# Ten modulation pieces summed during the even projection, by VectorE and GpSimd, instead of six by VectorE alone

## The chip, the core and the metric

The kernel runs on one core of a Trainium2 chip. The core has five engines, each with its own program: TensorE (PE in the profile, its weight loads PEld), VectorE (DVE), ScalarE (ACT), GpSimd (POOL) and SyncE (SP, which here only issues DMAs). They meet through semaphores: an instruction raises one when it is done, and another engine's program waits until it has reached a value. The metric is the device time of one execution in microseconds.

## The reference

The model is a two-layer backbone over 1024 latent tokens and 256 context tokens, with 1024 channels, all in float32. An even layer runs grouped-query attention beside a bidirectional mLSTM, an odd layer two other kinds of attention; both are followed by a mixture of 32 experts. Each layer is modulated by vectors that come from the conditioning vector alone:

```
mod_l = silu(c)     @ w_ada[layer] + b_ada[layer]      # six vectors of 1024 for latent tokens
mod_c = silu(c_ctx) @ w_ada[layer] + b_ada[layer]      # six for context tokens
sh1, sc1, g1, sh2, sc2, g2 = split(mod_l, 6)
h = rms_norm(x, g_mix[layer]) * (1 + sc1) + sh1        # what the mixer reads
```

`w_ada` is 1024 x 6144 for each of two layers, 48 MB together. The kernel cuts it into 24 pieces of 512 columns (1024 rows x 512 columns, 2 MB). A piece is a weighted sum over the rows: 8 row blocks of 128 rows, each scaled by its rows' values of silu(c) (kind 0) or silu(c_ctx) (kind 1), added up, and then summed over the 128 partitions.

## The kernel before, in words

The stages run one after the other: modulation, even projection, mLSTM, even attention, output projection, experts of layer 0, and the same for the odd layer. The 24 pieces of the modulation are spread over these stages.

- Pieces 0 to 3 (`EARLY`) are computed in the modulation stage on PE, since the projection needs them.
- Pieces 4 to 9 (`SUMMED = 6`, L145) are scaled and added over the row blocks by DVE during the even projection, for both kinds. What comes out (128 partitions x 512 columns for each piece and kind) goes to DRAM (`g.sum_dram`).
- The mLSTM stage begins with `units` (L765). A unit "sums" reads up to four of these from DRAM, and PE sums them over the partitions with the selecting matrix `sel`; a unit "whole" loads one of the pieces 10 to 15 (2 MB) and PE does the whole product (`ada_product`, L157). Four buffers take turns (`wa`, `buf`, L774), and eight units (`LATE`, L775) go through load, `product`, `ada_out` on ACT, and `turn`. The mLSTM's loop starts when all are through.
- Pieces 16 to 23 (`LAST`) are scaled and added by POOL during the even attention, for kind 0 alone: a `tensor_scalar` with a column of `g.cs` (L1309) and a `tensor_tensor` add (L1317) for each row block.

**The even projection (L366).** Ten tiles of 128 tokens, tile number 2i + h. `walk_tiles` unrolls the first and the last pair; the others run in a loop on each engine (DVE has its own loop of `SUMMED // 2 - 1` turns, then unrolled tiles). For a tile, PE does rows 0 and 1, `turn_qk` of the tile before, rows 2, `transposes` of the tile after, rows 3, and `channels`. `turn_qk` (L499) waits for `x_sq`, ACT's squares of the tile two further on, and for `z_dve`, DVE's `channels_out` of the tile. `transposes` (L459) waits for `xh_ready`, DVE's normalised tokens, and for `qt_dve`, DVE's `k_out`.

DVE does, in the order of its program (L699): the first half of a piece's sum (`summed`, half 0), `rows_out`, `k_out` of the tile before, `norm_rope`, `modulate` for the next tile, the second half of the sum, `channels_out`, and `normalise` for the tile two further on. `channels_out` and `modulate` read PSUM; `summed`, `norm_rope` and `normalise` read and write SBUF.

The weights for the sums come in `slabs`, one piece of two halves (4 row blocks, 1 MB each), which lies in the last 512 columns of `zT`; `acc`, two accumulators, lies in the last 512 columns of `qT`. Both places get their real contents only from tile 6 on, so ACT waits for the sums before it writes there (L579, L589). A half is loaded again when DVE is done with it (`slab_used`). SP issues these loads, the loads of the tokens (`x_load`, which waits for the transposes of an earlier tile) and the stores of the sums in one queue, in the order of L428 to L441.

POOL's program in this stage fills `y_dram`, the experts' output, with zeros: four DMAs of 4.6 MB (L451), issued when the input weights are in, and then a wait until they have landed.

Of the kernel before, what the change touches and what calls it, by code (L numbers as in the profile page):

```python
# [25 lines left out]
ALU = mybir.AluOpType  # L26
# [3 lines left out]
P = 128  # L30
# [3 lines left out]
T = SEQ + CTX  # L34
# [37 lines left out]
class Count:  # L72
# [11 lines left out]

    def but(self, n):

        return self.sem, self.base + self.k - n

    def turn(self, i, per):
# [54 lines left out]
LAST = range(NCHUNK - 8, NCHUNK)  # L144
SUMMED = 6  # L145

# [219 lines left out]
def even_project(nc, g, A, L):  # L366
# [5 lines left out]
    with nc.cleanup_on_exit():  # L372
# [19 lines left out]
        def s(name):  # L392
            return nc.alloc_semaphore("ep_" + name)
# [9 lines left out]
        slabs = L.zT[:, :, T - 512:T]  # L403
        acc = [L.qT[:, kind, T - 512:T] for kind in range(2)]
        slab_in, slab_used = [s("slab_in0"), s("slab_in1")], [s("slab_used0"), s("slab_used1")]
        acc_st = s("acc_st")
        c = Count(nc, "ep_dve_step")
        with nc.Block() as block:

            @block.sync  # L410
            def _(sp):
                def x_load(n):

                    sp.wait_ge(t_done, 2 * n + 2)
                    sp.dma_start(x[:, n % 2, :], A["x"][0, n * P:(n + 1) * P, :]).then_inc(x_in[n % 2], 16)

                def slab_load(n, half):
                    if n:
                        sp.wait_ge(slab_used[half], n)
                    col = (EARLY + n) * 512  # L420
                    sp.dma_start(slabs[:, 4 * half:4 * half + 4, :],
                                 A["w_ada"][0, half * 512:(half + 1) * 512, col:col + 512].rearrange("(k p) n -> p k n", p=P)).then_inc(slab_in[half], 16)

                def acc_store(n):
                    sp.wait_ge(slab_used[1], n + 1)
                    sp.dma_start(g.sum_dram[:, n, :, :], L.qT[:, 0:2, T - 512:T]).then_inc(acc_st, 16)
# [12 lines left out]
                for n in range(SUMMED + 2, NTL):  # L439
                    x_load(n)  # L440
                sp.wait_ge(acc_st, 16 * SUMMED)  # L441
# [12 lines left out]

# [82 lines left out]
            def _(act):  # L537
# [38 lines left out]
                def channels_out(i, h, halves=(0, 1)):  # L576

                    if h == 0 and not place_of(i, h)[0] and not place_of(i, h)[1]:
                        act.wait_ge(slab_used[1], i * 2)  # L579
                    for half in halves:  # L580
                        act.wait_ge(z_done, i * 4 + 2 * h + half + 1)
                        for cc in range(4 * half, 4 * half + 4):
                            m = act.activation(L.zT[:, cc, bass.ds(i * 256 + h * P, P)], ps_ab[:, h, half, (cc % 4) * P:(cc % 4) * P + P], ACT.Identity,
                                               scale=L.halfw[:, cc + 8:cc + 9], bias=L.halfw[:, cc + 24:cc + 25])
                        m.then_inc(z_act, 1)

                def q_out(i, h):
                    if h == 0 and not place_of(i, h)[0] and not place_of(i, h)[1]:
                        act.wait_ge(acc_st, i * 32)  # L589
# [31 lines left out]
            def _(dve):  # L621
# [54 lines left out]

                def summed(i, h, half):

                    n = i * 2 + h - 1
                    dve.wait_ge(slab_in[half], n * 16 + 16)  # L680
                    if half == 0 and not (isinstance(n, int) and n == 0):
                        dve.wait_ge(acc_st, n * 16)
                    for k in range(4 * half, 4 * half + 4):
# [8 lines left out]
                    dve.wait_ge(*c.now())  # L692
                    dve.sem_inc(slab_used[half], 1)

# [4 lines left out]
                def tile(i, h):  # L699
                    first, final, last, before, after = place_of(i, h)  # L700
                    sums = not first and not (isinstance(i, int) and i * 2 + h > SUMMED)
# [25 lines left out]
                tile(0, 1)  # L727
                turns = SUMMED // 2 - 1
                with dve.Fori(0, turns) as j:
# [9 lines left out]
def even_mlstm(nc, g, A, L):  # L739
# [4 lines left out]
    def s(name):  # L744
        return nc.alloc_semaphore("ml_" + name)

    with nc.cleanup_on_exit():
# [25 lines left out]
        wa.append(arena[:, 0:KD * 512].rearrange("p (k n) -> p k n", n=512))  # L773
        buf = lambda n: n % 4  # L774
        assert LATE == 8  # L775
        wt = nc.alloc_sbuf_tensor("ml_wt", [P, 2, BH, P], F32)
# [43 lines left out]
        with nc.Block() as block:  # L820

            @block.sync
            def _(sp):
# [9 lines left out]

                for n in range(6):
                    load(n)
# [3 lines left out]
                sp.dma_start(row_dram[1].rearrange("d r t -> (d r) t"), ai_row).then_inc(rows_out, 16)  # L839
                for n in range(6, LATE):  # L840
                    load(n)
                sp.wait_ge(rows_out, 32)
# [11 lines left out]
                def body(it, step, tiles):  # L854
                    if isinstance(it, int):
                        rows_in(0, step)
                        rows_in(1, step)
                        sp.wait_ge(ada_mm, LATE - 1)
                        for b in range(4):
                            values_in(b, tiles)  # L860
                        sp.wait_ge(ada_mm, LATE)
                        rows_in(2, step)
# [11 lines left out]
            def _(pool):  # L874
# [14 lines left out]
                def body(it, step, tiles):  # L889
                    for par in range(2):  # L890
                        for d in range(2):
                            b, tile = 2 * par + d, tiles(par)[d]
                            if isinstance(it, int) and it == 0:
                                pool.wait_ge(ada_mm, LATE - 3 + par)

# [117 lines left out]
            def _(act):  # L1013
# [30 lines left out]
                for cc in range(2, 8):  # L1044
                    gate(cc)
                    if cc < 6:
                        ada_out(cc)
                for n in range(6, LATE):
                    ada_out(n)
                act.wait_ge(tabs_ready, 1)  # L1050
# [21 lines left out]
            def _(dve):  # L1072
# [82 lines left out]
                dve.wait_ge(ada_turned, LATE)  # L1155
                for a, b in ((0, 4), (4, SUMMED)):
                    to = slice(4 * (EARLY + a), 4 * (EARLY + b))
# [2102 lines left out]
```

## Time and profile before

| | us |
|---|---|
| device time, median of 3 runs | 3146.27 (3143.32 to 3149.4) |
| the profiled execution | 3146.45 |
| its span, first to last instruction | 3144.5 |
| busy: PE / DVE / ACT / POOL | 2863.3 / 1480.4 / 1082.9 / 692.9 |
| mean granted clock of PE | 0.959 |

The profile is of one execution. A row of a timeline has the start in us from the span's start, the length, the engine, the line of the kernel, the operation, output and inputs, shapes and count; in brackets stands how long the engine was idle before it and what released it. Neighbouring instructions of one line are put together (x8). A row of grouped instructions has minimum, median and maximum in ns. The whole span in 40 slices of 78.6 us, each digit the busy share in tenths, shows the even projection in the second to fifth slice and the first half of the sixth:

```profile
PE   6999988899999689999987999899999959998895
DVE  2667436755554432222224677566665342232223
POOL 0000005799051033332221010000002013332233
PEclk8999988899999899999998999899999979999998
DMA  9722027433052399999984221200003459999997
```

### The profile page before, as it was taken

The page shows a single profiled execution, that of the slowest core. Times are in us where ns is not written, and L with a number is a line of the kernel's source. Part 1 is how long each engine was busy: PE and PEld are TensorE (multiplying, and loading weights), DVE is VectorE, ACT ScalarE, POOL GpSimd, SP SyncE. Part 2 cuts the span into 40 slices and gives each one's busy share as a digit, 9 for nine tenths or more (in the row PEclk, how much of TensorE's full clock was granted, in tenths as well). Part 3 has the DMA queues.
Part 4 walks back from the last instruction along what each step waited for, and adds up shares of the span by engine and source line. Part 5 has one row for each costly group of instructions (what it writes and reads, how often), then busy time and mean ns, then how long its engine had stood idle before and what let it go on. Part 6 is the DMA issues. An engine that isn't in the chain of part 4 may idle for free. (4 is left out here: it accounts for less than half of the span.)

```text
span 3144.5 us, 72871 instructions
## 1 busy us (share of the span) xinstructions
PE 2863.3 (91%) x27771; PEld 1889.6 (60%) x27771; DVE 1480.4 (47%) x4244; ACT 1082.9 (34%) x2480; POOL 692.9 (22%) x929
## 2 busy tenths in 40 slices
PE   6999988899999689999987999899999959998895
PEld 3666656745544357776663555577776537795573
DVE  2667436755554432222224677566665342232223
ACT  1222124466621123333333343455553103332232
POOL 0000005799051033332221010000002013332233
PEclk8999988899999899999998999899999979999998
DMA  9722027433052399999984221200003459999997
GB/s 371 276 91 77 20 102 231 116 112 100 1 181 88 158 376 414 413 416 417 418 355 155 84 82 66 74 1 1 1 1 116 154 222 384 418 416 417 418 417 300
DMA packets 167397, 665.00 MB, mean 211 GB/s; under 512 B 25373, under 2 KB 37929, under 8 KB 117621
## 3 DMA queue, kind: packets, MB, share of 16 engines
q1 hardware_dynamic: 136736, 574.30, 47.1%
q0 software_dynamic: 19456, 56.67, 5.1%
q10 hardware_dynamic: 10964, 30.68, 2.5%
q8 instruction: 170, 2.79, 0.4%
q14 instruction: 71, 0.57, 0.1%
HBM read 581.98 MB, written 86.90 MB: 213 GB/s over the span
## 5 line engine op out<-in xcount | busy, mean ns | idle before, releaser
L2877 PE MATMUL ps_g<-w_ring,work 128*32 128x256 f32 x7328 | 432.0, 382 | 26.5 <-DMA w_ring<-in_w 15.1
L2964 DVE STREAM_TRANSPOSE work<-work 128x256 f32<-128x256 f32 x189 | 123.6, 654 | 662.1 <-PE ps_g L2877 633.6
L2877 PEld LDWEIGHTS ps_g<-w_ring,work 128*32 128x32 f32 x7328 | 290.7, 110 | 138.5 <-issue 32.4
L2930 ACT COPY work<-ps_y 32x256 f32<-32x256 f32 x760 | 275.7, 363 | 285.0 <-PE ps_y L2892 278.2
L2877 PE MATMUL ps_g<-w_early,work 128*32 128x256 f32 x4640 | 281.4, 389 | 36.2 <-DMA w_early<-in_w 24.7
L2002 PE MATMUL of_ps_r<-w_early,cat 128*128 128x512 f32 (+1 forms) x608 | 255.9, 577 | 1.6 <-ACT cat L2084 1.6
L2877 PEld LDWEIGHTS ps_g<-w_early,work 128*32 128x32 f32 x4640 | 183.6, 112 | 113.3 <-issue 44.8
L484 PE MATMUL ps_r<-w,hT 128*128 128x512 f32 (+1 forms) x640 | 250.0, 547 | 1.5 <-ACT hT L554 1.5
L2825 POOL DMA_INDIRECT work<-f_dram,ex_idx x200 | 204.6, 1023 | 171.4 <-POOL ex_idx L2822 168.9
L2924 ACT ACTIVATE work<-ps_g 128x128 f32<-128x128 f32 x192 | 53.3, 277 | 515.8 <-PE ps_g L2877 509.1
L2892 PE MATMUL ps_y<-w_ring,work 128*32 128x256 f32 x3680 | 226.7, 380 | 3.4 <-ACT work L2930 3.4
L2833 POOL COPY work<-work 128x256 f32<-128x256 f32 x192 | 76.6, 399 | 535.7 <-DVE work L2964 395.2
L2002 PEld LDWEIGHTS of_ps_r<-w_early,cat 128*128 128x128 f32 x608 | 114.8, 192 | 124.6 <-issue 122.3
L484 PEld LDWEIGHTS ps_r<-w,hT 128*128 128x128 f32 x640 | 120.4, 192 | 114.8 <-issue 107.4
L1653 PE MATMUL mo_ps_o<-mo_w,mo_cT 128*128 128x512 f32 x416 | 185.8, 599 | 1.6 <-DMA mo_w<-in_e_w_out 0.9
L2892 PEld LDWEIGHTS ps_y<-w_ring,work 128*32 128x32 f32 x3680 | 150.1, 111 | 56.0 <-ACT work L2930 4.3
L2464 DVE TENSOR_SCALAR_CACHE_REDUCE w_early<-oa_ps_s 128x512 f32<-128x512 f32 (+1 forms) x288 | 159.0, 598 | 20.4 <-PE oa_ps_s L2378 17.8
L2433 ACT ACTIVATE w_early<-w_early,oa_mins 128x1280 f32<-128x1280 f32 x96 | 131.0, 1364 | 65.9 <-DVE oa_mins L2470 65.9
L495 PEld LDWEIGHTS ps_ab<-hT,w 128*128 128x128 f32 x1280 | 144.6, 192 | 4.8 <-issue 4.8
L495 PE MATMUL ps_ab<-hT,w 128*128 128x128 f32 x1280 | 144.7, 275 | 0.0
L2892 PE MATMUL ps_y<-w_early,work 128*32 128x256 f32 x2304 | 141.5, 381 | 0.0
L1653 PEld LDWEIGHTS mo_ps_o<-mo_w,mo_cT 128*128 128x128 f32 x416 | 78.9, 192 | 100.5 <-issue 98.0
(509 smaller groups left out, 4432.7 us busy)
## 6 DMA issues: line engine op xcount, KB each, us to landing
w_ring<-in_w SPq DMA_DIRECT2D x232, 1024.0 KB, 25.2
w_early<-in_w SPq DMA_DIRECT2D x152, 1024.0 KB, 25.4
y_dram<-work ACTq DMA_DIRECT2D x190, 128.0 KB, 5.9
y_dram<-zeros POOLq DMA_DIRECT2D x4, 4608.0 KB, 27.2
ea_slab<-in_w_ada SPq DMA_DIRECT2D x64, 256.0 KB, 2.9
zT<-in_w_ada SPq DMA_DIRECT2D x12, 1024.0 KB, 6.0
f_dram<-mo_f SPq DMA_DIRECT2D x18, 512.0 KB, 2.9
w<-in_e_w_in SPq DMA_DIRECT2D x2, 4096.0 KB, 20.4
```

What stands on the lines that cost most here:

```text
L484: mm = pe.matmul(ps_r[:, n, 0:cols[1] - cols[0]], hT[:, h, k, :], w[:, k, cols[0]:cols[1]], start=k == 0, stop=k == KD - 1)
L495: mm = pe.matmul(ps_ab[:, h, half, (cc % 4) * P:(cc % 4) * P + P], w[:, k, Z0 + cc * P:Z0 + (cc + 1) * P], hT[:, h, k, :], start=k == 0, s ...
L1653: mm = pe.matmul(ps_o[:, half * 512:(half + 1) * 512], row, w[:, k, half * 512:(half + 1) * 512], start=k == 0, stop=k == KD - 1)
L2002: mm = pe.matmul(ps_r[:, bank[m], 0:b - a], hT[:, n % 2, k, :], w[:, k, a:b], start=k == 0, stop=k == KD - 1)
L2433: act.activation(sx[:, n % 3, part, :], sx[:, n % 3, part, :], ACT.Exp, scale=-1.0, bias=mins[:, n % 3, part, 3:4], accum_out=sums[:, n % ...
L2464: dve.tensor_scalar(sx[:, n % 3, part, a:b], ps_s[:, k % 2, part, 0:b - a], -SCALE[units[n][1]], BIG, ALU.mult, ALU.min, accum_out=mins[:, ...
L2825: pool.indirect_dma_start(out=xg[:, at * 256:(at + 1) * 256], out_offset=None, in_=R.f_dram.rearrange("t (q d) -> (t q) d", q=QU), in_offs ...
L2833: pool.tensor_copy(xs, xg[:, at * 256:(at + 1) * 256]).then_inc(x_ready, 1)
L2877: mm = pe.matmul(ps_h[rows, :], xT[:, k * UNIT:(k + 1) * UNIT], w[:, :, kk * DE + n * P:kk * DE + (n + 1) * P], start=k == 0, stop=k == KD ...
L2892: mm = pe.matmul(ps_y[n * UNIT:(n + 1) * UNIT, :], hT[:, k * UNIT:(k + 1) * UNIT], w[:, kk, n * 256:(n + 1) * 256], start=k == 0, stop=k == 3)
L2930: w = act.copy(y[b * UNIT:(b + 1) * UNIT, n * 256:(n + 1) * 256], ps_y[n * UNIT:(n + 1) * UNIT, :])
L2964: dve.transpose(xT.rearrange("p (k t) -> p k t", k=KD), xs.rearrange("p (r k) -> p k r", k=KD)).then_inc(x_turned, 1)
```

## The change

`SUMMED` becomes 10: the even projection sums pieces 4 to 13. DVE does kind 0 of each piece and POOL kind 1, from the same slab. DVE does two pieces in each of the tiles 1 to 5, one at the beginning of the tile and one before `channels_out`, with one accumulator, and so waits for its own last operation each time. [...] POOL's accumulator has two buffers. A half of the slab is loaded again when both engines are done with it. SP's order is new: the load of the next half 0, DVE's store, the load of the next half 1, POOL's store, and after every second piece a load of tokens.

The mLSTM stage has five units instead of eight: two "sums" of four pieces, two "whole" (pieces 14 and 15), one "sums" of two pieces; the waits on `ada_mm` that name units follow.

```diff
-SUMMED = 6
+SUMMED = 10
...
                 for n in range(SUMMED):
-                    if n + 1 < SUMMED:
-                        slab_load(n + 1, 0)
-                    x_load(n + 2)
-                    acc_store(n)
-                    if n + 1 < SUMMED:
-                        slab_load(n + 1, 1)
-                for n in range(SUMMED + 2, NTL):
-                    x_load(n)
+                    slab_load(n + 1, 0)
+                    dve_store(n)
+                    slab_load(n + 1, 1)
+                    pool_store(n)
+                    if n % 2 == 0:
+                        x_load(n // 2 + 2)
+                x_load(SUMMED // 2 + 2)
...
+                for n in range(SUMMED):
+                    to = acc_pool[n % 2]
+                    for half in range(2):
+                        pool.wait_ge(slab_in[half], 16 * n + 16)
+                        if half == 0 and n > 1:
+                            pool.wait_ge(pool_st[n % 2], 16 * (n // 2))
+                        for k in range(4 * half, 4 * half + 4):
+                            pool.tensor_scalar(product if k else to, slabs[:, k, :], L.cs[:, k, 1:2], None, ALU.mult).then_inc(*pool_step.up())
+                            pool.wait_ge(*pool_step.now())
+                            if k:
+                                pool.tensor_tensor(to, to, product, ALU.add).then_inc(*pool_step.up())
+                                pool.wait_ge(*pool_step.now())
+                        pool.sem_inc(used_pool[half], 1)
                 pool.wait_ge(filled, 64)
...
                 def channels_out(i, h, halves=(0, 1)):
                     if h == 0 and not place_of(i, h)[0] and not place_of(i, h)[1]:
-                        act.wait_ge(slab_used[1], i * 2)
+                        act.wait_ge(used_dve[1], i * 4 - 2)
+                        act.wait_ge(used_pool[1], i * 4 - 2)
...
-                def summed(i, h, half):
+                def summed(i, h, second):
-                    n = i * 2 + h - 1
+                    n = i * 4 + 2 * h - 2 + second
...
-                        for kind in range(2):
-                            by = L.cs[:, k, kind:kind + 1]
+                            by = L.cs[:, k, 0:1]
                             if k == 0:
-                                m = dve.tensor_scalar(acc[kind], slabs[:, k, :], by, None, ALU.mult)
+                                m = dve.tensor_scalar(acc, slabs[:, k, :], by, None, ALU.mult)
                             else:
-                                dve.wait_ge(*c.but(1))
-                                m = dve.scalar_tensor_tensor(out=acc[kind], in0=slabs[:, k, :], scalar=by, in1=acc[kind], op0=ALU.mult, op1=ALU.add)
+                                dve.wait_ge(*c.now())
+                                m = dve.scalar_tensor_tensor(out=acc, in0=slabs[:, k, :], scalar=by, in1=acc, op0=ALU.mult, op1=ALU.add)
...
-        units = [("sums", 0, 4)] + [("whole", q) for q in range(whole, whole + 3)] + [("sums", 4, SUMMED)] + [("whole", q) for q in range(whole + 3, LAST[0])]
+        units = [("sums", 0, 4), ("sums", 4, 8)] + [("whole", q) for q in range(whole, LAST[0])] + [("sums", 8, SUMMED)]
```

## Rows read from the trace of the kernel before

**Rows 1.** Busy us in 40 us: PE, PEld, DVE, ACT, POOL, clock, DMA.
```profile
152.00:192.00 40.00, 40.00 (x206) 27.78 (x205) 26.28 (x71) 7.92 (x18) 0.00 (x0) 1.00 0.28 92
```

**Rows 2.** Timeline of PE, tiles 1 and 2 of the even projection.
```profile
105.65 1.04 PE L467 MATMUL ps_ab<-consts_sb,x 128*128 128x128 f32 x8
...
138.22 0.60 PE L514 MATMUL ps_ab<-consts_sb,sq 128*128 128x128 f32 x4
...
145.63 1.04 PE L467 MATMUL ps_ab<-consts_sb,x 128*128 128x128 f32 x8
```

**Rows 3.** Timeline of DVE, tile 2 of the even projection.
```profile
140.96 0.29 DVE L697 COPY kT<-ps_ab 128x128 f32 x1
...
151.05 5.38 DVE L690 SCALAR_TENSOR_TENSOR qT<-zT,cs,qT 128x512 f32<-128x512 f32 x8
162.44 0.30 DVE L665 COPY edges<-ps_ab 128x4 f32 x2 [6.00 <-ACT zT L583]
...
163.98 1.12 DVE L673 SCALAR_TENSOR_TENSOR zT<-ps_ab,halfw,zT 128x127 f32 x4
169.60 0.29 DVE L665 COPY edges<-ps_ab 128x4 f32 x2 [4.50 <-ACT zT L583]
...
173.54 0.15 DVE L626 TENSOR_SCALAR xs<-xs 128x1 f32<-128x1 f32 x1 [1.30 <-ACT ps_ab L546]
```

**Rows 4.** Instructions on the tile zT: min/median/max ns, starts.
```profile
L690 DVE SCALAR_TENSOR_TENSOR qT<-zT,cs,qT x84: 743/748/751, 96.1 to 315.7; 128x512 f32<-128x512 f32 x84
```

**Rows 5.** Timeline of POOL, even projection: issues of the fills.
```profile
63.68 5.73 POOL L451 DMA_DIRECT2D y_dram<-zeros  x3 [21.48 <-DMA w<-in_e_w_in]
...
117.21 1.83 POOL L451 DMA_DIRECT2D y_dram<-zeros  x1 [47.80 <-issue]
```

**Rows 6.** POOL's lines L1309, L1317, L1614 (min/median/max ns), then its timeline.
```profile
L1309 POOL TENSOR_SCALAR ea_slab<-ea_slab,cs x64: 1553/1564/1579, 608.6 to 781.2; 128x512 f32<-128x512 f32 x64
...
L1317 POOL TENSOR_TENSOR ea_slab<-ea_slab x56: 1261/1272/1289, 611.8 to 782.8; 128x512 f32<-128x512 f32 x56
...
L1614 POOL TENSOR_SCALAR qT<-qT x10: 612/617/1599, 892.4 to 951.2; 128x512 f32<-128x512 f32 x10
...
618.79 1.56 POOL L1309 TENSOR_SCALAR ea_slab<-ea_slab,cs 128x512 f32<-128x512 f32 x1
620.43 1.26 POOL L1317 TENSOR_TENSOR ea_slab<-ea_slab 128x512 f32<-128x512 f32 x1
621.68 1.56 POOL L1309 TENSOR_SCALAR ea_slab<-ea_slab,cs 128x512 f32<-128x512 f32 x1
```

**Rows 7.** Timelines of POOL and DVE after the even attention.
```profile
895.47 1.29 POOL L1610 TENSOR_TENSOR hb<-hb,gbc 128x512 f32<-128x512 f32 x1
895.66 1.13 DVE L119 TENSOR_TENSOR mo_s<-mo_s,mo_ss 128x16 f32<-128x16 f32 x1
...
920.75 2.11 POOL L1616 TENSOR_TENSOR hb<-hb,qT 128x512 f32<-128x512 f32 x1
921.77 2.17 DVE L1818 TENSOR_TENSOR mo_f<-mo_f,mo_rows 128x1024 f32<-128x1024 f32 x1
```

**Rows 8.** DMA issues, 130 to 330 us: KB, median us to landing.
```profile
zT<-in_w_ada SPq DMA_DIRECT2D x8, 1024.0 KB, 5.4
```

**Rows 9.** Timelines of SP, POOL and PE, head of the mLSTM stage.
```profile
452.64 0.34 SPq L830 DMA_DIRECT2D ml_staging<-sum_dram  x1
...
485.87 3.52 SPq L848 DMA_DIRECT2D ml_spare<-ml_rows  x4
...
492.18 1.38 POOL L886 MEMSET hb<- 128x1536 f32 x1 [33.66 <-DVE zT L1078]
...
498.84 3.64 PE L157 MATMUL ml_ps_c<-ml_arena,cs 128*32 128x512 f32 x16 [3.12 <-DMA ml_arena<-in_w_ada]
...
500.30 0.20 POOL L900 COPY ml_cur<-ml_tab 128x16 f32<-128x16 f32 x1 [6.74 <-DMA ml_spare<-ml_rows]
...
505.85 2.05 PE L974 MATMUL ml_ps_s<-ml_staging 128*128 128x128 f32 x8
```

More of the change, by code:

```diff
@@ L403, in even_project @@
         slabs = L.zT[:, :, T - 512:T]
-        acc = [L.qT[:, kind, T - 512:T] for kind in range(2)]
-        slab_in, slab_used = [s("slab_in0"), s("slab_in1")], [s("slab_used0"), s("slab_used1")]
-        acc_st = s("acc_st")
+        acc, acc_pool, product = L.qT[:, 0, T - 512:T], [L.qT[:, n, T - 512:T] for n in (1, 3)], L.qT[:, 2, T - 512:T]
+        slab_in = [s("slab_in0"), s("slab_in1")]
+        used_dve, used_pool = [s("used_dve0"), s("used_dve1")], [s("used_pool0"), s("used_pool1")]
+        dve_st, pool_st = s("dve_st"), [s("pool_st0"), s("pool_st1")]
+        pool_step = Count(nc, "ep_pool_step")
         c = Count(nc, "ep_dve_step")
@@ L417, in slab_load, with dve_store, pool_store @@
                 def slab_load(n, half):
+                    if n >= SUMMED:
+                        return
                     if n:
-                        sp.wait_ge(slab_used[half], n)
-                    col = (EARLY + n) * 512
+                        sp.wait_ge(used_dve[half], n)
+                        sp.wait_ge(used_pool[half], n)
+                    layer, col = (EARLY + n) // (NCHUNK // 2), (EARLY + n) % (NCHUNK // 2) * 512
                     sp.dma_start(slabs[:, 4 * half:4 * half + 4, :],
[L422 to L426, printed above, removed]
+                                 A["w_ada"][layer, half * 512:(half + 1) * 512, col:col + 512].rearrange("(k p) n -> p k n", p=P)).then_inc(slab_in[half], 16)
+                def dve_store(n):
+                    sp.wait_ge(used_dve[1], n + 1)
+                    sp.dma_start(g.sum_dram[:, n, 0, :], acc).then_inc(dve_st, 16)
+                def pool_store(n):
+                    sp.wait_ge(used_pool[1], n + 1)
+                    sp.dma_start(g.sum_dram[:, n, 1, :], acc_pool[n % 2]).then_inc(pool_st[n % 2], 16)
                 x_load(0)
@@ L432, in _ @@
                 for n in range(SUMMED):
-                    if n + 1 < SUMMED:
-                        slab_load(n + 1, 0)
-                    x_load(n + 2)
-                    acc_store(n)
-                    if n + 1 < SUMMED:
-                        slab_load(n + 1, 1)
-                for n in range(SUMMED + 2, NTL):
-                    x_load(n)
-                sp.wait_ge(acc_st, 16 * SUMMED)
+                    slab_load(n + 1, 0)
[5 more added lines that the diff above has]
+                x_load(SUMMED // 2 + 2)
+                sp.wait_ge(dve_st, 16 * SUMMED)
+                for b in range(2):
+                    sp.wait_ge(pool_st[b], 8 * SUMMED)
             @block.gpsimd
@@ L588, in q_out @@
                     if h == 0 and not place_of(i, h)[0] and not place_of(i, h)[1]:
-                        act.wait_ge(acc_st, i * 32)
+                        act.wait_ge(dve_st, i * 64 - 32)
+                        for b in range(2):
+                            act.wait_ge(pool_st[b], i * 32 - 16)
                     act.wait_ge(qt_done, i * 2 + h + 2)
@@ L675, in channels_out @@
                         m.then_inc(z_dve, 1)
-                def summed(i, h, half):
-                    n = i * 2 + h - 1
[L680 to L683, printed above, removed]
-                        for kind in range(2):
-                            by = L.cs[:, k, kind:kind + 1]
+                def summed(i, h, second):
+                    n = i * 4 + 2 * h - 2 + second
+                    for half in range(2):
+                        dve.wait_ge(slab_in[half], n * 16 + 16)
+                        if half == 0 and not (isinstance(n, int) and n == 0):
+                            dve.wait_ge(dve_st, n * 16)
+                        for k in range(4 * half, 4 * half + 4):
+                            by = L.cs[:, k, 0:1]
                             if k == 0:
-                                m = dve.tensor_scalar(acc[kind], slabs[:, k, :], by, None, ALU.mult)
+                                m = dve.tensor_scalar(acc, slabs[:, k, :], by, None, ALU.mult)
                             else:
-                                dve.wait_ge(*c.but(1))
-                                m = dve.scalar_tensor_tensor(out=acc[kind], in0=slabs[:, k, :], scalar=by, in1=acc[kind], op0=ALU.mult, op1=ALU.add)
+                                dve.wait_ge(*c.now())
+                                m = dve.scalar_tensor_tensor(out=acc, in0=slabs[:, k, :], scalar=by, in1=acc, op0=ALU.mult, op1=ALU.add)
                             m.then_inc(*c.up())
-                    dve.wait_ge(*c.now())
-                    dve.sem_inc(slab_used[half], 1)
+                        dve.wait_ge(*c.now())
+                        dve.sem_inc(used_dve[half], 1)
                 def k_out(i, h):
@@ L700, in tile @@
                     first, final, last, before, after = place_of(i, h)
-                    sums = not first and not (isinstance(i, int) and i * 2 + h > SUMMED)
+                    sums = not first and not (isinstance(i, int) and i * 2 + h > SUMMED // 2)
                     if sums:
@@ L727, in _ @@
                 tile(0, 1)
-                turns = SUMMED // 2 - 1
+                turns = SUMMED // 4
                 with dve.Fori(0, turns) as j:
@@ L773, in even_mlstm @@
         wa.append(arena[:, 0:KD * 512].rearrange("p (k n) -> p k n", n=512))
-        buf = lambda n: n % 4
-        assert LATE == 8
+        buf = lambda n: (n + 1) % 4
+        assert LATE == 5
         wt = nc.alloc_sbuf_tensor("ml_wt", [P, 2, BH, P], F32)
@@ L832, in load @@
                         ada_load(sp, A, units[n][1], wa[buf(n)], ada_in[buf(n)])
-                for n in range(6):
+                for n in range(LATE):
                     load(n)
@@ L839, in _ @@
                 sp.dma_start(row_dram[1].rearrange("d r t -> (d r) t"), ai_row).then_inc(rows_out, 16)
-                for n in range(6, LATE):
-                    load(n)
                 sp.wait_ge(rows_out, 32)
@@ L1045, in _ @@
                     gate(cc)
-                    if cc < 6:
+                    if cc < LATE:
                         ada_out(cc)
-                for n in range(6, LATE):
-                    ada_out(n)
                 act.wait_ge(tabs_ready, 1)
@@ L1155, in _ @@
                 dve.wait_ge(ada_turned, LATE)
-                for a, b in ((0, 4), (4, SUMMED)):
+                for a, b in ((0, 4), (4, 8), (8, SUMMED)):
                     to = slice(4 * (EARLY + a), 4 * (EARLY + b))
```

8 lines of the change are left out of this document (3 added, 5 removed).

## The prediction, on record before the result

> **What bounds the kernel now.** I read the stretches of the even projection first, since most of the change is there, then the engines' timelines in them, then the place where GpSimd already does the same kind of sum, and last the head of the mLSTM stage. In a 40 us stretch of the projection PE is busy all 40.00 us at a granted clock of 1.00, DVE 26.28 us, POOL not at all, and the DMA engines 0.28 of the time [rows 1]. A token tile takes 40.0 us: the transposes (L467) of one tile begin at 105.65, of the next at 145.63 [rows 2]. So PE is the bound there, and whatever PE has to wait is added to the end. PE waits for DVE at two places in a tile: `turn_qk` (L503) wants the squares of a later tile, which come after DVE's `channels_out`, and `transposes` wants DVE's `k_out` of the tile before, which stands right behind the first sum. Today `k_out` is done at 141.2, 4.4 us early, and DVE has slack: in a tile it waits 6.00, 4.50 and 1.30 us for ACT [rows 3].
>
> The head of the mLSTM stage is bound otherwise: PE's last product waits for its slab until 498.84, POOL's first staging copy waits until 500.30 for table rows that queue behind the slabs, and the first scores begin at 505.85, 53 us after the stage's first load at 452.64 [rows 9].
>
> **POOL's new work.** Ten pieces, each of 8 multiplies and 7 adds of 128x512, every one waiting for the one before. The same two instructions stand in the even attention: the multiply by a column of `cs` takes 1.56 us (64 of them, 1553 to 1579 ns), the add 1.27 us. A dependent add starts 1.64 us after its multiply, and the following multiply, which does not depend on it, 1.25 us after the add [rows 6]. With a wait after every instruction I take 1.64 and 1.33 (the same 0.08 us for the wait). Half a slab is then 4 x 1.64 + 3 x 1.33 = 10.6 us and the second half 4 x 2.97 = 11.9 us: 22.4 us a piece, 44.9 us for the two pieces of a tile, against 40.0 us of PE. POOL alone is thus too slow already.
>
> It also starts late. POOL first issues the four fills of `y_dram`; three go out from 63.68, but the fourth only at 117.21 for 1.83 us [rows 5], so the first multiply can't start before 119.0 (perhaps 115, if the fill drains faster with one slab load fewer beside it).
>
> **What both engines cost each other.** Where POOL and DVE work on SBUF together (the gate products after the even attention), they take turns. DVE's L1818 is issued at 921.77 and ends at 923.94, and POOL's L1616, issued at 920.75, ends at 922.86: each runs after the other's end, POOL's in 2.11 instead of 1.27 us. From the end of L1616 to the end of L1818 is 1.08 us for 1024 columns. A small DVE operation, L119, takes 1.13 us, though it has only 16 columns: it ends just after POOL's L1610, which had begun before it [rows 7]. The new sums are two-input SBUF operations like L1818, and so are nearly all of `norm_rope`. So I take it that they exclude each other. [...]
>
> DVE's own path through a tile: 40.0 less its waits (11.8) and plus 1.3 for the squares is 29.5 us. The sums in it are two eights of 5.38 us, 10.8; with one accumulator instead of two each of the 16 must wait for the one before, 0.75 + 0.04 = 0.79 us, 12.6 in all [rows 3, 4]. That makes 31.3 us. POOL adds 16 x 1.56 + 14 x 1.27 = 42.8 us of instructions. I take it that POOL can run without holding DVE while DVE reads PSUM (in the attention, where DVE does, POOL's rows hardly vary [rows 6]) or waits for ACT: `channels_out` some 5 (each half like 162.44 to 165.1), the squares 1.3, `modulate` about 1.1 (four operations, as L673's), `rows_out`, `k_out` and the reduction some 1.8, in all 9.2 us. An instruction that has waited for the other engine has its start behind it (1.13 after the hand-over instead of 1.27; on DVE 0.54 for 512 columns instead of 0.75): 30 x 0.14 and about 12 x 0.2, together 6.6 us. The tile becomes 31.3 + 42.8 - 9.2 - 6.6 = 58.3 us, 18.3 more than PE needs. Without exclusion it would be POOL's 44.9, and with no overlap at all 74; I take 58, which the rows of taking turns give.
>
> **The first tiles, step by step.** DVE sums piece 0 from 96 [rows 4], but piece 1 needs the slab back. POOL ends the first half of piece 0 at 129.6; the load of 1 MB lands 5.4 us later [rows 8], 135.0. POOL ends the second half at 141.5, and 2.2 us later since DVE's first four operations fall into it: 143.7; that load lands at 149.1. DVE's piece 1 ends at 156.4, `channels_out` at 161.3, the squares at 162.6, the normalising (2.3 us, and two POOL instructions, 4.9) at 167.5. Then piece 2, eight operations that each let one POOL instruction pass, 8 x (0.54 + 1.28) = 14.6, and `k_out`: 182.9. PE's transposes were at 145.63, so they are 37 us late. In the next tile both pieces run against POOL for their whole length, 64.7 us, then come two tiles of 58.3: 24.7 + 36.6 = 61 us more. After the last of these `k_out`, DVE still needs some 38 us to the squares (58.3 less 14.6 for the sum, 0.8, and 4.9 for the normalising), PE from its transposes to `turn_qk` 32.6 (105.65 to 138.22 [rows 2]): 5.5 us beyond that. The projection becomes longer by 37 + 61 + 5.5 = 104 us, with bounds of 42 and 142 from the rivals below. PE stands still for some microseconds before it goes on; after the last such wait I add 2 us for a lower clock, an estimate: half of the 3.64 us of the product at 498.84, which runs right after a wait [rows 9].
>
> **Other edits.** SP's order: `x_load` now stands behind `pool_store`, and so behind POOL, which puts the load of tile 4's tokens at about 144; they are read after two more tiles, some 80 us later, so nothing. Queued behind SP's waits are only the next slab halves, which wait for the same POOL. The slab traffic grows from 12 to 20 MB and the stores from 3 to 5 MB: the DMA engines were at 0.28 [rows 1], so nothing; were they full, 8 MB would cost some 20 us. ACT's new waits before `channels_out` and `q_out` ask for pieces that POOL ends 10 us or more earlier: nothing. POOL's wait for the fill now stands behind the sums: nothing.
>
> **The head of the mLSTM stage.** Five units instead of eight, 9 MB instead of 15. The slabs are there some 18 us earlier. Next late is the chain of gates on ACT and DVE, which loses one `ada_out` (0.6 us and its wait): about 2 us earlier, so POOL's clearing at 492.18 comes at 490.2 and ends at 491.6. The table rows, issued at 485.87 because their stores queued behind slabs, come at about 482 and land with nothing ahead of them before 490. So POOL stages from 491.6 instead of 500.30, and PE, no longer turning the last piece until 505.85, follows after 3.8 us, at 495.4: 10 us gained [rows 9]. Bounds: 2 (the gates alone) and 18 (all that the slabs free).
>
> **Sum.** The profiled execution took 3146.45 us (its span 3144.5), 0.2 from the median of the three runs, 3146.27. 3146.45 + 104 + 2 - 10 = 3242 us.
>
> **Rivals.** First, the engines don't exclude each other in these forms and POOL alone is the bound. Then DVE's piece 8 ends 119.0 + 8 x 22.4 + 5.4 + 3.2, and `k_out` 0.8 later at 307.6, against 265.6 (145.63 and three tiles): +42, less 10: 3179 us. For it: the 64 multiplies of the attention hardly vary though DVE is busy beside them. Against it: that DVE reads PSUM there, and rows 7.
>
> Second, the turns cost full price and each piece shows a slab landing: 31.3 + 42.8 - 9.2 + 6 = 71 us a tile, 37 + 3 x 31 + 12 = 142, in all 3146 + 142 - 10 = 3278 us. For it: small operations on DVE may each wait for a whole POOL instruction, and a tile has some 20.
>
> Third, on the other side: POOL's piece is cheap enough to hide. The multiply with two immediates (L1614) takes 617 ns [rows 6]; at that price a piece is 8 x 0.62 + 7 x 1.27 = 13.9 us, and without exclusion only the late start is left, 119.0 + 2 x 13.9 + 9.4 - 145.6 = 10.6 us. With the full 18 us at the mLSTM head this gives 3139 us. It decides at about 17 us a piece, where the later tiles would begin to wait. [...] Against it too: exclusion would add to every piece.
>
> **How the numbers follow.** The forecast 0.70, its own range 3210 to 3270 by the start at 115 or 119 and by 54 to 64 us a tile; the first rival 0.10, the second 0.14, the third 0.04, and a sum of such parts that comes to nothing 0.02. The range 3175 to 3290 takes in the first two rivals. What can be told from no change here is 0.2%, about 6 us: slower 0.94, within it 0.02, faster 0.04.
>
> **What would show it.** Right: PE idle before L467 and `turn_qk` in four or five tiles of the projection, tiles of 55 to 65 us there, DVE's L690 at well above 0.75 us, POOL's new adds above 1.27 us, the mLSTM stage beginning near 558 instead of 452.6, and some 43 us from there to the first scores. POOL's multiplies at 1.56 us with tiles of 45 us would show the first rival, multiplies near 0.6 us and no idle PE the third. The prediction is wrong if DVE's sums keep 0.75 us beside POOL, or if POOL starts long before 115.

## The result and the profile after

The changed kernel takes 3200.56 us (median of 4 runs, 3199.02 to 3204.45) against 3147.84 us (4 runs, 3143.32 to 3149.56): ratio 1.0171, 95% interval 1.0159 to 1.0183, or 52.7 us more. The prediction had the sign and the place, and 96 us. The measured time lies in its range of 3175 to 3290, but below the 3210 to 3270 of the forecast itself. The profiled execution is the longest of the four, 3204.45 us (span 3202.7).

PE in the even projection of the changed kernel (start, length; in brackets the idle time before and who ended it) answers to [rows 2]; the line of the transposes is now L486:

```profile
103.20 1.04 PE L486 MATMUL ps_ab<-consts_sb,x 128*128 128x128 f32 x8
...
153.88 1.11 PE L533 MATMUL ps_ab<-consts_sb,sq 128*128 128x128 f32 x4 [17.94 <-ACT ps_ab L565]
...
173.42 1.94 PE L486 MATMUL ps_ab<-consts_sb,x 128*128 128x128 f32 x8 [8.99 <-DVE kT L719]
223.90 1.94 PE L486 MATMUL ps_ab<-consts_sb,x 128*128 128x128 f32 x8 [8.60 <-DVE kT L719]
274.14 1.94 PE L486 MATMUL ps_ab<-consts_sb,x 128*128 128x128 f32 x8 [8.00 <-DVE kT L719]
324.64 1.94 PE L486 MATMUL ps_ab<-consts_sb,x 128*128 128x128 f32 x8 [7.79 <-DVE kT L719]
367.54 1.04 PE L486 MATMUL ps_ab<-consts_sb,x 128*128 128x128 f32 x8
```

Before, these transposes stood 39.98 us apart. Now the first distance is 70.2 us (30.2 late), three are 50.2 to 50.5, the next is 42.9. Next comes a stretch of 40 us, to be read beside [rows 1]. Below it stands what DVE waited for from 160 to 360 us and POOL from 100 to 400 us (us in total, times, longest):

```profile
158.00:198.00 40.00, 31.01 (x167) 22.16 (x166) 29.47 (x42) 4.71 (x12) 37.44 (x24) 0.85 0.39 126
```
```profile
DVE qT L712 <- DMA zT<-in_w_ada: 33.1, 8, 6.8
```
```profile
POOL qT L466 <- POOL qT L469: 4.4, 19, 0.3
```

POOL is busy 37.44 of 40 us and, once begun, never waits for data, only for itself, at most 0.3 us at a time. DVE waits 33.1 us in eight waits, 4 us each, for the next half of a slab, which is loaded when POOL lets go of the old one. So in these tiles POOL is the bound, not DVE. Its instructions and DVE's sums (min, median, max in ns; beside [rows 6] and [rows 4]):

```profile
L466 POOL TENSOR_SCALAR qT<-zT,cs x80: 1562/1568/2014, 114.5 to 360.6; 128x512 f32<-128x512 f32 x80
...
L469 POOL TENSOR_TENSOR qT<-qT x70: 1259/1270/1867, 117.9 to 362.2; 128x512 f32<-128x512 f32 x70
...
L712 DVE SCALAR_TENSOR_TENSOR qT<-zT,cs,qT x70: 750/1059/1643, 93.4 to 348.2; 128x512 f32<-128x512 f32 x70
```

The mLSTM stage begins at 514.66 instead of 452.64 (+62.0); to the first scores it takes 44.65 us instead of 53.21 [rows 9]:

```profile
514.66 0.32 SPq L852 DMA_DIRECT2D ml_staging<-sum_dram  x1
```
```profile
559.31 2.08 PE L994 MATMUL ml_ps_s<-ml_staging 128*128 128x128 f32 x8 [9.37 <-POOL ml_staging L926]
```

62.0 - 8.6 = 53.4 us, which accounts for the 52.7 between the medians. The two profiled executions lie 58.0 us apart; the other 4.7 us come after the first scores. Runs of one kernel differ by 5 to 6 us, so I leave them unexplained.

### The profile page after: what moved, and what is told of

Its sections match the earlier page's. It is cut to its first block and busy times, and to the rows that moved or that the text cites. A ratio compares the mean times of both kernels' runs of the same rounds, so it can differ in the third digit from the quotient of the medians.

```text
span 3202.7 us, 72957 instructions
## 1 busy us (share of the span) xinstructions
PE 2874.2 (90%) x27699; PEld 1896.1 (59%) x27699; DVE 1522.4 (48%) x4229; ACT 1081.6 (34%) x2477; POOL 923.5 (29%) x1079
## 3 DMA queue, kind: packets, MB, share of 16 engines
q1 hardware_dynamic: 138192, 578.49, 46.7%
## 5 line engine op out<-in xcount | busy, mean ns | idle before, releaser
L2895 PEld LDWEIGHTS ps_g<-w_ring,work 128*32 128x32 f32 x7328 | 291.9, 111 | 137.2 <-issue 33.1
L2895 PE MATMUL ps_g<-w_early,work 128*32 128x256 f32 x4640 | 282.4, 389 | 35.1 <-DMA w_early<-in_w 23.7
L503 PE MATMUL ps_r<-w,hT 128*128 128x512 f32 (+1 forms) x640 | 257.1, 559 | 1.5 <-ACT hT L573 1.5
L2910 PEld LDWEIGHTS ps_y<-w_ring,work 128*32 128x32 f32 x3680 | 150.8, 111 | 56.5 <-issue 4.5
L1626 POOL TENSOR_TENSOR cat<-cat,mo_rs 128x512 f32<-128x512 f32 x8 | 10.4, 1306 | 481.7 <-DVEq L1811 481.7
## 6 DMA issues: line engine op xcount, KB each, us to landing
w_ring<-in_w SPq DMA_DIRECT2D x232, 1024.0 KB, 23.7
```

Source lines behind the costliest of these rows:

```text
L503: mm = pe.matmul(ps_r[:, n, 0:cols[1] - cols[0]], hT[:, h, k, :], w[:, k, cols[0]:cols[1]], start=k == 0, stop=k == KD - 1)
L2895: mm = pe.matmul(ps_h[rows, :], xT[:, k * UNIT:(k + 1) * UNIT], w[:, :, kk * DE + n * P:kk * DE + (n + 1) * P], start=k == 0, stop=k == KD ...
L2910: mm = pe.matmul(ps_y[n * UNIT:(n + 1) * UNIT, :], hT[:, k * UNIT:(k + 1) * UNIT], w[:, kk, n * 256:(n + 1) * 256], start=k == 0, stop=k == 3)
```

## The experiments

Theory A: POOL's own chain sets the pace of the tiles. Theory B, as predicted: DVE's path does, held up by the whole length of every POOL instruction. Each total is given with its ratio to the kernel before on the same chip. Runs 1, 3, 8 and 10 change values, so later stages see other values; there the start of the mLSTM stage tells more than the total.

**1. No sums on POOL.** POOL clears both accumulators and only signals.

```diff
-                        for k in range(4 * half, 4 * half + 4):
-                            pool.tensor_scalar(...) ... pool.tensor_tensor(...)
```

> The changed kernel without GpSimd's 150 multiplies and adds: GpSimd clears its two accumulators once, stores these zeros ten times and keeps all its signals. So the second row of ten pieces is zero, later stages see other values, and the starts of stages are read beside the total. Theory A (GpSimd's own chain of 22.4 us a piece, stretched to 25.1 by VectorE, sets the projection's pace) and theory B (as predicted: VectorE's own path, lengthened by the whole length of every GpSimd instruction, sets it) both expect no wait of TensorE left in the projection, mLSTM's first head product at about 453 to 456 us in place of 514.66, its head 8.6 us shorter than in the kernel before, and a total of about 3139 us. A rival C, that the larger traffic of slabs and stores or the code around the sums costs a good part of the 62 us, expects the projection to stay 10 us or more late and the total at 3150 or more.

3148.92 us (1.0003, 0.9993 to 1.0013); mLSTM begins at 464.39, +11.75. PE's transposes and DVE's second piece:

```profile
103.71 1.04 PE L483 MATMUL ps_ab<-consts_sb,x 128*128 128x128 f32 x8
...
156.89 1.07 PE L483 MATMUL ps_ab<-consts_sb,x 128*128 128x128 f32 x8 [0.33 <-DVE kT L716]
196.91 1.04 PE L483 MATMUL ps_ab<-consts_sb,x 128*128 128x128 f32 x8
```
```profile
133.57 0.48 DVE L706 TENSOR_SCALAR qT<-zT,cs 128x512 f32<-128x512 f32 x1 [23.48 <-DMA sum_dram<-qT]
```

Both theories missed 13.2 us at the third tile, which here come without any arithmetic on POOL; the later tiles are back at 40. POOL's first signal still stands behind the fills, SP's store of DVE's first piece stands behind the slab load that waits for this signal, and DVE, with one accumulator, waits for the store. That store also travels slowly, beside the last fill. SP's issues, and the stores' time to landing between 90 and 140 us and between 160 and 300 us:

```profile
115.89 0.37 SPq L422 DMA_DIRECT2D zT<-in_w_ada  x1
116.30 1.52 SPq L427 DMA_DIRECT2D sum_dram<-qT  x1
```
```profile
sum_dram<-qT SPq DMA_DIRECT2D x2, 256.0 KB, 18.1
```
```profile
sum_dram<-qT SPq DMA_DIRECT2D x14, 256.0 KB, 3.2
```

By these rows the 13.2 us have two parts, which no run separates: the signal comes at 115.9, and the store then takes 17 us instead of 3. The other 17 of the 30 us, and all growth, need POOL's sums.

**2. Fills behind the sums.** The four DMAs of `y_dram` are issued after POOL's sums.

> The changed kernel with GpSimd's four fills of the expert rows issued behind its sums in place of ahead of them: its first multiply can start about 45 us earlier (about 70 us in place of 114.53), and nothing else changes. Theory A (GpSimd's chain, 25.1 us a piece from its first instruction on): TensorE's wait of 30 us at its third tile goes nearly whole, what is left grows by some 10 us a tile as GpSimd falls behind, the projection ends about 22 to 25 us later than before in place of 62, total about 3164 us. Theory B (VectorE's path, about 50 us for each tile in which it meets GpSimd, whenever GpSimd starts): the tile after the first is now slowed as well, so 10 us are paid five times, the projection ends about 50 us late, total about 3188 us.

3167.19 us (1.0064, 1.0046 to 1.0082): A's 3164, not B's 3188. mLSTM begins at 479.68, +27.0. PE's transposes:

```profile
104.24 1.04 PE L486 MATMUL ps_ab<-consts_sb,x 128*128 128x128 f32 x8
145.41 1.06 PE L486 MATMUL ps_ab<-consts_sb,x 128*128 128x128 f32 x8 [1.02 <-DVE kT L719]
189.26 1.89 PE L486 MATMUL ps_ab<-consts_sb,x 128*128 128x128 f32 x8 [3.68 <-DVE kT L719]
239.48 1.94 PE L486 MATMUL ps_ab<-consts_sb,x 128*128 128x128 f32 x8 [8.37 <-DVE kT L719]
```

The first distance is only 1.2 us longer than before although POOL already works beside it (busy 38.44 of 41 us); POOL's lead is used up first, and then the tiles take 50 us again. The late start was worth 33 us of the loss.

**3. Constant instead of column.** `slabs[:, k, :], 0.5, None, ALU.mult`.

> The changed kernel with GpSimd's 80 multiplies by the constant 0.5 in place of a column of the condition (the second row of ten pieces has other values, so the starts of stages are read beside the total); the multiply then takes about 0.62 us (as other multiplies by constants of this tile in the trace) in place of 1.56, a piece 13.9 in place of 22.4. The fills stay ahead of the sums. Theory A: GpSimd keeps up with a tile of 40 us, so only its late start is left: +17 to +30 us at the third tile and no further growth; total about 3156 to 3169 us. Theory B by the full length of every GpSimd instruction: 27.8 us per tile hold VectorE in place of 42.8, tile 43 to 46 us, growth of 3 to 6 us a tile behind the same first delay; total about 3170 to 3185 us.

3202.02 us (1.0178, 1.0159 to 1.0197); mLSTM begins at 509.14, +56.5. The premise failed: this multiply still takes 1510 ns (median of 80), so the run tells nothing between A and B. See 9 and 10.

**4 to 6. POOL's instructions beside the kernel before.** On buffers of their own, from 120 us on, read by nobody:

```diff
+                for n in range(120):     # 4: multiplies; 5: 140 adds; 6: 64 pairs
+                    pool.tensor_scalar(pa, pc, L.cs[:, n % 8, 1:2], None, ALU.mult).then_inc(*pool_step.up())
+                    pool.wait_ge(*pool_step.now())
```

> The kernel before, with 120 multiplies by a column of the condition on GpSimd, in its own buffers, from about 119 us on (187 us of them); nothing reads them, VectorE, its six pieces and its slabs are as before. [...] Theory A' (the column multiply holds VectorE out only for about its first 0.65 of 1.56 us): VectorE's path stays near the 40 us of TensorE's tile; 0 to 8 us, total 3147 to 3156. Theory B (every GpSimd instruction holds VectorE out for its whole length): 25 us more on VectorE's path in each tile, some 17 us a tile for 4 tiles, +60 to +75, total about 3215.

> The kernel before, with 140 adds of two tiles on GpSimd (178 us of them), in its own buffers, from about 119 us on; nothing reads them. The add holds VectorE out for its whole 1.27 us by theory A' and by theory B, so both expect a clear loss: VectorE's path 48 to 56 us a tile for 3.5 to 4.5 tiles, +35 to +70 us, total 3183 to 3218. What tells A' from B is that it loses several times what the multiplies alone lose (A'), or as much (B).

> The kernel before, with 64 pairs of a column multiply and an add on GpSimd (181 us alone, some 200 with what it loses to VectorE), in its own buffers, from about 119 us on; nothing reads them. It is the changed kernel's mix of instructions without its dependences. Theory A (in the changed kernel GpSimd's own chain sets the pace, and VectorE has some 6 us a tile to spare): VectorE's path 44 us a tile, +4 us a tile, about +20 (10 to 35), total 3158 to 3183. Theory B (VectorE's path sets it): as in the changed kernel, 10 us a tile for 4 tiles at least, or by the full exclusion of the prediction 18.6 us a tile, +40 to +80, total 3188 to 3228.

Multiplies: 3147.62 us (0.9999, 0.9989 to 1.0008). Adds: 3218.89 (1.0217, 1.0200 to 1.0234). Pairs: 3161.85 (1.0036, 1.0023 to 1.0049). DVE's groups between 150 and 310 us follow (after the bar busy us and mean ns of one), with multiplies, adds and pairs. They are the sums, where both tensors lie in SBUF, and in the first two a group with one input in PSUM; with adds also the first multiply of a sum, which reads one tensor, from SBUF:

```profile
L701 DVE SCALAR_TENSOR_TENSOR qT<-zT,cs,qT 128x512 f32<-128x512 f32 x56 | 45.8, 883 | 0.0
...
L684 DVE SCALAR_TENSOR_TENSOR zT<-ps_ab,halfw,zT 128x127 f32 x32 | 9.0, 342 | 1.1
```
```profile
L701 DVE SCALAR_TENSOR_TENSOR qT<-zT,cs,qT 128x512 f32<-128x512 f32 x36 | 59.8, 1727 | 0.0
...
L698 DVE TENSOR_SCALAR qT<-zT,cs 128x512 f32<-128x512 f32 x4 | 5.7, 1465 | 1.3 <-issue 1.3
L684 DVE SCALAR_TENSOR_TENSOR zT<-ps_ab,halfw,zT 128x127 f32 x20 | 5.6, 342 | 0.7
```
```profile
L703 DVE SCALAR_TENSOR_TENSOR qT<-zT,cs,qT 128x512 f32<-128x512 f32 x50 | 56.7, 1200 | 0.0
```

A sum of 748 ns [rows 4] becomes 883 beside multiplies that run without a break and 1727 beside adds. The operations that read PSUM keep 342 ns even there. In the run with pairs, POOL's mix without its dependences, a tile takes 42.5 to 45.3 us: that is DVE's path by itself, some 6 us short of the 50 of the changed kernel. (Its sums have two accumulators; the prediction put one accumulator at 1.8 us a tile more.) B's 58.3 and its +40 to +80 are refuted by 4 and 6; A is held up.

**7 and 11. DVE alone, ten pieces.** The twenty half pieces in tiles 1 to 6 as 3, 4, 4, 4, 3, 2, two sets of accumulators; fills behind (7) or ahead (11).

```diff
+        acc = [[L.qT[:, 2 * b + kind, T - 512:T] for kind in range(2)] for b in range(2)]
+        units_of = {1: (1, 2, 0), 2: (1, 2, 1), 3: (1, 2, 1), 4: (1, 2, 1), 5: (1, 2, 0), 6: (1, 1, 0)}
...
+                    for v in range(b):
+                        summed(u + a + v)
...
+                    elif m:
+                        channels_out(i, h, (0,))
+                        summed(u + a + b)
+                        channels_out(i, h, (1,))
```

> A version that is to beat both: ten pieces, both rows by VectorE alone, GpSimd without any sum; 20 half pieces (5.4 us each in the trace of before) in tiles 1 to 6 as 3, 4, 4, 4, 3, 2 in place of 2 a tile, the further ones put where VectorE waited 6.0 us and 4.5 us for ScalarE in a tile; two sets of accumulators; the fills behind the last piece; mLSTM's head as in the changed kernel. Theory A: what cost time was GpSimd's chain and its late start, and VectorE had the room, 11.8 us of waits a tile for 5.4 to 10.8 us more of sums; TensorE waits for 0 to 6 us in the whole projection, the head of mLSTM gives 8.6 us back, total 3139 to 3145 us. Rival: a tile with four half pieces leaves VectorE no room (31.3 + 10.8 us of path against 40), some 3 us late in three tiles, and the slabs' loads come late besides; the 8.6 us are used up, total 3148 or more.

> The version with ten pieces by VectorE alone, but with the fills of the expert rows at their old place, ahead, about 64 to 117 us. It tells whether the fills' place matters where GpSimd sums nothing. Case one: the slabs' loads and stores of the first tiles go through the fills' traffic (0.92 of the DMA engines' time between 78 and 118 us), the second piece comes late, TensorE waits some 13 us at its third tile, as it did with GpSimd's sums left out, total about 3150 us. Case two: those 13 us came from GpSimd's signal, which stood behind the fills, and not from the traffic; TensorE waits for nothing or 1 to 3 us, total 3138 to 3141 us.

3137.54 us (0.9971, 0.9958 to 0.9983) and 3137.42 us (0.9961, 0.9947 to 0.9976): both faster than both kernels. PE of run 7, and a stretch with four half pieces in a tile:

```profile
143.62 1.04 PE L472 MATMUL ps_ab<-consts_sb,x 128*128 128x128 f32 x8
183.61 1.04 PE L472 MATMUL ps_ab<-consts_sb,x 128*128 128x128 f32 x8
```
```profile
158.00:198.00 40.00, 40.00 (x208) 27.81 (x207) 36.42 (x88) 7.92 (x18) 0.00 (x0) 1.00 0.47 155
```

DVE is busy 36.42 of 40 us and PE still 40.00: the waits of [rows 3] held the sums. The mLSTM head takes 42.05 us (run 11: 46.79). In run 11 the fills stand ahead again and PE waits for nothing, so their traffic alone (0.98 of the DMA engines' time between 78 and 118 us) costs nothing: DVE's own signal sends the first slab load out at 99.85. (Its second set of accumulators also spares DVE the wait for the store.) In run 1 that load waited for POOL's signal, until 115.89, and only then did the traffic of the last fill matter.

**8. No sums on DVE.** It clears its accumulator and keeps its waits and signals.

> The changed kernel without VectorE's sums: it clears its accumulator once, keeps its waits and signals; the first row of ten pieces is zero, so later stages see other values and the projection is what is read. GpSimd's sums are whole. Theory A (GpSimd's chain sets the pace): a tile still takes 44.9 to 47 us (two pieces of 22.4 us and what the rest of VectorE's work costs it), TensorE's transposes stand 44.9 to 47 us apart from the third tile on. Theory B (VectorE's path sets the pace, 50.2 us a tile as measured): 12 us of sums leave each tile, 38 us are left, and TensorE's 40 us a tile come back; after the first delay nothing grows.

PE's transposes:

```profile
168.10 1.94 PE L486 MATMUL ps_ab<-consts_sb,x 128*128 128x128 f32 x8 [8.31 <-DVE kT L711]
216.56 1.94 PE L486 MATMUL ps_ab<-consts_sb,x 128*128 128x128 f32 x8 [6.49 <-DVE kT L711]
264.88 1.94 PE L486 MATMUL ps_ab<-consts_sb,x 128*128 128x128 f32 x8 [6.69 <-DVE kT L711]
```

48.3 to 48.9 us a tile: without 12 us of DVE's work only 1.8 us go. That is A (a little above its 47) and excludes B's return to 40. The total is 3180.54 us (1.0108).

**9 and 10. A cheap multiply.** `L.cs[:, k, 1:2], 0.0, ALU.mult, ALU.add` (9; values as before) and `0.5, 0.25, ALU.mult, ALU.add` (10).

> The changed kernel with GpSimd's multiply written with two operations, times the column of the condition and plus 0.0, in place of one operation (every value stays). The only cheap multiply in the trace of before, 617 ns, had two operations with two constants; one constant alone took 1.51 us in the run before this one. Two cases. Two operations make the multiply cheap: 0.62 us, a piece of 13.9 us in place of 22.4, GpSimd is no longer the bound; its late start stays (13 us at the third tile without any sums) and the 14 adds of a tile hold VectorE for 17.8 us: a tile of 40 to 43 us, total 3155 to 3175 us. Only constants make it cheap: the multiply stays at 1.5 us or more, tile 49 to 50 us, total about 3200 us.

> The changed kernel with GpSimd's 80 multiplies replaced by times 0.5 plus 0.25, two constants, the form of the 617 ns in the trace of before (the second row of ten pieces has other values, so the starts of stages are read beside the total). This is the shortening that the run with one constant was to be. Theory A (GpSimd's chain sets the pace): a piece of 13.9 us, GpSimd idle for a third of each tile, the tile 40 to 43 us, the start of mLSTM 20 to 35 us later than in the kernel before in place of 62. Theory B (VectorE's path, held for the whole length of every GpSimd instruction, 27.8 us a tile): 43 to 46 us, the start of mLSTM 40 us later.

Run 9: 3181.27 us (1.0106, 1.0088 to 1.0123); mLSTM begins 44.8 us late. Its multiply, and what POOL waited for between 60 and 360 us:

```profile
L466 POOL TENSOR_SCALAR qT<-zT,cs x80: 692/700/1339, 115.6 to 322.4; 128x512 f32<-128x512 f32 x80
```
```profile
POOL qT L466 <- DMA zT<-in_w_ada: 28.3, 8, 7.4
```

The same product with a second operation takes 0.70 us instead of 1.56. The wait changes sides: now POOL waits for slabs and DVE for none. Tiles fall to 48.2, 46.7 and 45.5 us, not to the 40 to 43 expected; 21.4 us of the 44.8 are the first delay, where DVE waits 23.7 us for its store as in run 1. In run 10 (632 ns; 3198.30 us, 1.0159) the tiles take 46.7 to 45.0 us and mLSTM begins 40.0 us late, which is B's number, not A's. So once POOL's chain is short, DVE's path, held by the adds, is the bound. Theory A holds for the kernel as changed, with a bound on DVE's side only some 3 to 6 us below.

## Why the prediction was right or wrong

- **What bounds the projection before, and that PE would idle:** right. PE waits at the two places named, once at `turn_qk` and four times at the transposes.
- **POOL's piece, 22.4 us, and its start at 119 "(perhaps 115)":** 114.5, and 80 multiplies and 70 adds (137.3 and 95.5 us busy, 16.2 between) make 24.9 us a piece, 2.5 us more than forecast: 1.9 in instructions that last longer beside DVE than in [rows 6], 0.6 in pauses.
- **The step that failed: "POOL adds 16 x 1.56 + 14 x 1.27 = 42.8 us of instructions" to DVE's path, a tile of 58.3 us.** The 25 us of multiplies in it hardly count: 120 of them cost no time in run 4 (a sum rose from 748 to 883 ns), while 140 adds cost 70 us. [Rows 7], from which I took the exclusion, show POOL's adds and products of two tensors alone. With the true hold DVE's path is about 44 us (run 6), POOL's chain 44.9 + 5 for what DVE takes from it, and POOL sets the pace: 10.5, 10.3 and 10.5 us of growth where 24.7, 18.3 and 18.3 were forecast. That the time still fell into the range is luck as far as the mechanism goes: the range had been drawn to take in the rival "POOL alone". The operation of DVE before those of [rows 7] and that of POOL after them, in the kernel before:

```profile
920.13 1.60 DVE L1815 SCALAR_TENSOR_TENSOR mo_f<-zT,mo_xs,mo_rows 128x1024 f32<-128x1024 f32 x1
...
922.82 2.02 POOL L1608 TENSOR_TENSOR hb<-hb,mo_rs 128x512 f32<-128x512 f32 x1
```

POOL's L1616 ends at 922.86, 1.13 us after DVE's L1815 (921.73). DVE's L1818 ends 1.08 us after L1616, and POOL's L1608 0.90 us after L1818, in 2.02 instead of 1.04 us.

- **The first delay, 37 us:** 30.2. DVE's second and third piece in the changed kernel:

```profile
135.84 0.49 DVE L709 TENSOR_SCALAR qT<-zT,cs 128x512 f32<-128x512 f32 x1 [26.24 <-DMA sum_dram<-qT]
136.37 3.51 DVE L712 SCALAR_TENSOR_TENSOR qT<-zT,cs,qT 128x512 f32<-128x512 f32 x3
143.07 4.46 DVE L712 SCALAR_TENSOR_TENSOR qT<-zT,cs,qT 128x512 f32<-128x512 f32 x4 [3.19 <-DMA zT<-in_w_ada]
...
167.92 4.30 DVE L712 SCALAR_TENSOR_TENSOR qT<-zT,cs,qT 128x512 f32<-128x512 f32 x4 [6.72 <-DMA zT<-in_w_ada]
```

The store that "Other edits" priced at nothing holds DVE until 135.84, but the slab that POOL releases comes later still, and again for the third piece. POOL's first two pieces end at 162.3, the slab lands at 167.9, and DVE's four sums and `k_out` end at 173.3. The forecast had DVE's eight sums taking turns with POOL there, until 182.9. So this delay is POOL's chain too; the store sets it only where that chain is short or gone (runs 1 and 9).
- **End, 5.5 + 2 us:** 2.9 at the last distance. PE waits for nothing in it, so the 5.5 did not come. PE only runs slower after its last wait: the granted clock was 0.50 from 324.6 to 328 us and 0.69 to 332, and 1.00 after. (Over the product at 498.84 in the kernel before it was 0.50.) The stage also began 2.4 us earlier. 30.2 + 31.3 + 2.9 - 2.4 = 62.0 against 106.
- **mLSTM head, -10 us:** -8.6. In the other kernels with the new head and true values it took 41.4 to 46.8 us.
- **Rivals:** the first had the bound right (POOL alone) but, without any exclusion, 3179 us. With the measured start and piece its sum comes out: 114.5 + 8 x 24.9 + 5.4 + 3.2 + 0.8 = 323.1, and the transposes begin at 324.64. What it lacked was mainly the 2.5 us a piece. The third had the cheap multiply that run 9 found, yet not the adds' hold, and put the first delay at 10.6 us where run 9 has 21.4; the time stayed 33 us above before.

The forecast left `channels_out` free of POOL, as inferred from the attention; no row of the kernel before shows it for these lines. Run 5 does: DVE's operations that read PSUM take 342 ns beside adds, 343 in the kernel before. Reading only one tensor from SBUF keeps nothing free there: the first multiply of a sum does so and takes 1465 ns instead of 482. In the changed kernel L113, 0.17 us long elsewhere, ends with the add that it meets, and L122 ends 0.8 us before the multiply that it meets, as the last part shows.

## What to carry to other kernels

Before work is moved to a second engine, add up that engine's own chain for one period and compare it with the period: 44.9 against 40 us already settled the sign here. The size came from the late start (33 us, run 2) and from what POOL loses beside DVE (24.9 us a piece for 22.4). A chain below the period would not have been enough: in run 9 POOL waited for slabs, and the kernel was still 33 us slower than before. Look for room on the engine that has the data already: the waits in its timeline, 11.8 us a tile, held the additional sums. Any signal that is to come from an engine comes after all that stands ahead in its program, here 44 us of waiting to issue the last fill.

## What was not expected of the hardware

GpSimd's one-operation multiply lets VectorE's operations on two SBUF tensors in before it ends. VectorE and GpSimd in the changed kernel:

```profile
226.02 0.57 DVE L308 TENSOR_SCALAR hn_ss<-hn_ss 128x10 f32<-128x10 f32 x1
...
226.84 1.11 DVE L113 TENSOR_TENSOR hn_s<-hn_r 128x10 f32<-128x10 f32 x1
...
228.19 0.55 DVE L122 SCALAR_TENSOR_TENSOR hn_s<-hn_s 128x10 f32<-128x10 f32 x1
228.76 0.17 DVE L124 SCALAR_TENSOR_TENSOR hn_r<-hn_s,hn_r 128x10 f32<-128x10 f32 x1
228.97 0.17 DVE L113 TENSOR_TENSOR hn_s<-hn_r 128x10 f32<-128x10 f32 x1
```
```profile
224.66 1.90 POOL L466 TENSOR_SCALAR qT<-zT,cs 128x512 f32<-128x512 f32 x1 [0.21 <-POOL qT L469]
226.65 1.27 POOL L469 TENSOR_TENSOR qT<-qT 128x512 f32<-128x512 f32 x1
228.02 1.57 POOL L466 TENSOR_SCALAR qT<-zT,cs 128x512 f32<-128x512 f32 x1
```

L113 of 0.17 us lasts until the add ends (227.95 and 227.92). Beside the multiply, L122 ends at 228.74, 0.72 us after its start, and the next ones take their usual 0.17 us while it still runs for 0.8 us. 0.7 us is also the whole length of the two-operation form (0.70).

Not every form gets in. L308, which reads one SBUF tensor of 10 columns and takes 0.17 us alone (at 101.63), here takes 0.57 and ends with the multiply (226.59 and 226.56); so it does in all four tiles in which it meets one. What the rest of the 1.56 us holds is thus only inferred from such rows, and depends on VectorE's operation; why one operation takes longer than two is open.
